# A two-mixer decoder trunk: the low parts of the second mixer's input weights made by another engine, and its inverse spread in other helpings

## The reference

```python
proj = h @ w_in
qkv, z, beta_logit, a_logit = jnp.split(proj, ...)
qkv = jax.nn.silu(causal_depthwise_conv(qkv, conv_w))        # four taps
q, k, v = jnp.split(qkv, ...); q = l2_norm(q) * dk ** -0.5; k = l2_norm(k)
decay_mat = jnp.exp(jnp.where(causal, g_i - g_j, -inf))      # g: cumulative log decay in a chunk
m = jnp.where(strict, (k * beta) @ k.T * decay_mat, 0.0)
u, w = triangular_solve(m, [v * beta, k * beta * exp(g)])    # unit lower triangular, 64 x 64
# then a scan over 16 chunks of 64 rows (and first the 16 meta rows) with state s
v_new = u - w @ s;  o = q_dec @ s + a_qk @ v_new;  s = s * tot + k_dec.T @ v_new
out = (rms_norm(o, head_norm) * silu(z)) @ w_out
```

## Time and profile before

| | us |
|---|---|
| median of 3 executions | 1534.98 |
| lowest and highest | 1532.82, 1536.03 |
| profiled execution, its own time | 1536.11 |
| span of its instructions | 1534.3 |

### The profile page before, as it was taken

The page is one execution under the profiler, slowest core; times in us unless marked ns, Lnnn a source line. Parts: engine busy times, 40 slices in busy tenths (PEclk is TensorE's granted clock), DMA queues, the critical chain, the costliest instruction groups (busy, mean ns, idle before and its releaser), DMA issues.

```text
span 1534.3 us, 21430 instructions
## 1 busy us (share of the span) xinstructions
PE 1444.4 (94%) x8490; PEld 1211.2 (79%) x8490; DVE 789.5 (51%) x1017; ACT 429.0 (28%) x914; POOL 381.4 (25%) x303
## 2 busy tenths in 40 slices
PE   6999999975999999999999989999998999999997
PEld 4777779973788779999999988978886667777775
DVE  4213612222444437654556799989933654444432
ACT  4322832103222214333332422212222531111111
POOL 3212123415111112221221221222343342222200
PEclk9999999997999999999999999999999999999998
DMA  5520214526645314345345232235359794555530
GB/s 186 176 83 28 98 55 125 160 105 228 191 166 171 121 55 115 92 113 137 101 118 197 70 84 72 70 97 179 109 189 240 199 253 135 147 148 155 155 83 28
DMA packets 213853, 200.81 MB, mean 131 GB/s; under 512 B 62840, under 2 KB 177032, under 8 KB 213504
## 3 DMA queue, kind: packets, MB, share of 16 engines
q1 hardware_dynamic: 207168, 187.99, 41.1%
q10 hardware_dynamic: 6592, 11.54, 2.8%
HBM read 132.39 MB, written 67.09 MB: 130 GB/s over the span
## 4 chain that ended last, share of the span: by engine, by line
PE 42%; DVE 13%; issue 3%; ACT 3%; DMA 2%; ACTq 0%; POOLq 0%; DVEq 0%; SPq 0%; POOL 0%
PE banks L2564 11%; PE banks L1898 11%; PE banks L1832 9%; DVE gdn L2102 6%; PE banks L2644 2%; PE banks L2612 2%; PE banks L2614 2%; DVE gdn L2099 1%; PE banks L1726 1%; DMA gdn<-in_gdn_w_out 1%; PE banks L1750 1%; PE banks L2630 1%; PE banks L2623 1%; DVE gdn L2107 1%; ACT gdn L1966 1%
## 5 line engine op out<-in xcount | busy, mean ns | idle before, releaser
L1832 PE MATMUL banks<-hn_hi,gdn 128*128 128x352 f32 x1488 | 303.6, 329 | 0.0
L1832 PEld LDWEIGHTS banks<-hn_hi,gdn 128*128 128x128 f32 x1488 | 243.9, 190 | 4.1 <-issue 2.7
L2077 POOL TENSOR_TENSOR gdn<-gdn,gdn 128x1024 fp32r<-128x1024 f32 x31 | 99.8, 3220 | 316.8 <-ACT gdn L1934 316.8
L2102 DVE SCALAR_TENSOR_TENSOR gdn<-gdn,conv_taps,gdn 128x1040 f32<-128x1040 f32 x96 | 162.2, 1689 | 3.4
L1898 PE MATMUL banks<-gdn,hn_hi 128*128 128x512 f32 x512 | 161.8, 396 | 0.4 <-DVE gdn L2109 0.4
L1832 PE MATMUL banks<-hn_lo,gdn 128*128 128x352 f32 x744 | 159.1, 322 | 0.0
L1832 PEld LDWEIGHTS banks<-hn_lo,gdn 128*128 128x128 f32 x744 | 126.7, 189 | 0.0
L1898 PEld LDWEIGHTS banks<-gdn,hn_hi 128*128 128x128 f32 x512 | 95.5, 188 | 26.3 <-issue 2.6
L750 PE MATMUL ai_p<-ai_whi,hn_hi 128*128 128x512 f32 x264 | 106.0, 402 | 5.5 <-DVE ai_wlo L575 2.5
L750 PE MATMUL ai_p<-ai_wlo,hn_hi 128*128 128x512 f32 x264 | 104.8, 397 | 0.0
L750 PE MATMUL ai_p<-ai_whi,hn_lo 128*128 128x512 f32 x264 | 104.3, 395 | 0.0
(11 more groups left out here) (287 smaller groups left out, 2477.1 us busy)
## 6 DMA issues: line engine op xcount, KB each, us to landing
gdn<-in_gdn_w_in SPq DMA_DIRECT2D x32, 512.0 KB, 4.1
ai_st<-in_gla_w_in SPq DMA_DIRECT2D x32, 256.0 KB, 4.7
gdn_kq<-gdn SPq DMA_DIRECT2D x16, 512.0 KB, 3.9
gdn_v<-gdn SPq DMA_DIRECT2D x16, 512.0 KB, 3.5
gdn<-in_gdn_w_in SPq DMA_DIRECT2D x32, 256.0 KB, 4.6
gdn<-gdn_kq SPq DMA_DIRECT2D x16, 512.0 KB, 3.7
gdn<-gdn_ek SPq DMA_DIRECT2D x16, 512.0 KB, 5.3
gdn<-gdn_v SPq DMA_DIRECT2D x32, 256.0 KB, 6.7
```

Source lines behind the costliest of these rows:

```text
L1832: last = pe.matmul(a[:, b, 0:m], w[n % 2][:, kt, :], x[:, kt, PAD + s:PAD + s + m], start=(kt == 0 and e == 0), stop=(kt == KT - 1 and e = ...
L2077: pool.tensor_tensor(lo[n % 2][:, :, :], st[n % 2][:, :, :], hi[n % 2][:, :, :].bitcast(F32), ALU.subtract).then_inc(S("ni_wlo"), 1)
L2102: dve.scalar_tensor_tensor(cv[:, :], xs[:, tap:tap + L], T.cw[:, tap, t:t + 1], cv[:, :], ALU.mult, ALU.add).then_inc(S("ni_conv"), 1)
```

## The change

Four edits. The low parts of tiles 4 to 32 are made by VectorE, in window n for tile n + 1, behind its other work of that window (for odd n up to 17 also behind both copies of `ev_k`) and ahead of the inverse; every wait on a low part of these tiles now counts `ni_wlo_v`. The preparatory work is cut up: the distances are done in windows 18 and 19, the exponents' second half (`differences`) moves from window 21 to 22, ScalarE's `exps` from window 22 to 23. The inverse begins in window 24, not 23, with a budget of 2800, not 4200. In the scan, the load of the second chunk's decay factors goes behind the first scan matrices, and 6 of the 16 fillers behind the meta products go ahead of them.

```diff
--- before.py
+++ after.py
@@ -1574,17 +1574,24 @@
                 return NQK + head_of_k(n) * P
             return 2 * NQK + v_of(n) * P
 
+        def lo_made(eng, n):
+
+            if n < 4:
+                wait(eng, S("ni_wlo"), n - 1)
+            else:
+                eng.wait_ge(S("ni_wlo_v"), n - 3)
+
         def sync(sp, ahead):
             def load(n):
                 wait(sp, S("ni_whi"), n - 3)
-                wait(sp, S("ni_wlo"), n - 3)
+                lo_made(sp, n - 2)
                 sp.dma_start(st[n % 2][:, :, :], wv[:, :, col(n):col(n) + P]).then_inc(S(f"ni_w_in{n % 2}"), 16)
 
             def load_z(p_):
                 if p_ < 4:
                     last = NIN - 2 + p_ // 2
                     sp.wait_ge(S("ni_whi"), last - 1)
-                    sp.wait_ge(S("ni_wlo"), last - 1)
+                    lo_made(sp, last)
                 elif p_ < NZ * KT - 4:
                     sp.wait_ge(S("ni_zhi"), p_ - 3)
                     sp.wait_ge(S("ni_zlo"), p_ - 3)
@@ -1817,7 +1824,7 @@
 
             def mm(n):
                 pe.wait_ge(S("ni_whi"), n - 1)
-                pe.wait_ge(S("ni_wlo"), n - 1)
+                lo_made(pe, n)
                 if n % 2 == 0:
                     wait(pe, S("ni_free0"), 3 * (n // 2))
                 else:
@@ -2039,7 +2046,7 @@
                     act.activation(sst[:, :], trA[0:NH * TT, 0, :], ACT.Copy).then_inc(S("ni_sse"), 1)
                 if n == v_tile(4):
                     logs()
-                if n == v_tile(5):
+                if n == v_tile(6):
                     exps()
 
             for n in range(NIN):
@@ -2084,7 +2091,7 @@
 
             for j in range(2):
                 pool.memset(tok[j][:, :, :], 0.0).then_inc(S("ni_tok_zero"), 1)
-            for n in range(2, NIN):
+            for n in range(2, 4):
                 split_lo(n)
             for p_ in range(NZ * KT):
                 z_lo(p_)
@@ -2101,6 +2108,11 @@
                     dve.wait_ge(S("ni_conv"), CONV * m + tap)
                     dve.scalar_tensor_tensor(cv[:, :], xs[:, tap:tap + L], T.cw[:, tap, t:t + 1], cv[:, :],
                                              ALU.mult, ALU.add).then_inc(S("ni_conv"), 1)
+
+            def split_lo(n):
+                dve.wait_ge(S("ni_whi"), n - 1)
+                dve.tensor_tensor(lo[n % 2][:, :, :], st[n % 2][:, :, :], hi[n % 2][:, :, :].bitcast(F32),
+                                  ALU.subtract).then_inc(S("ni_wlo_v"), 1)
 
             def tokens_out(buf, b, sem):
                 if b < 2:
@@ -2145,7 +2157,9 @@
                 b_ = be[:, half * L // 2:(half + 1) * L // 2]
                 dve.reciprocal(b_, b_).then_inc(S("ni_beta"), 1)
 
-            def distances():
+            HALVES = ((slice(0, 32), slice(0, C)), (slice(32, C), slice(32, C)))
+
+            def distances(n):
 
                 dve.wait_ge(S("ni_gs_in"), 48)
                 dve.wait_ge(S("ni_sct"), 3 * NH)
@@ -2153,10 +2167,12 @@
                     dve.wait_ge(S(f"ni_kq_out{j}"), 16 * NH)
                 gr = gs[:, 0:1, :]
                 gc = gs[:, 0, :].rearrange("p (j o) -> p j o", o=1)
-                for n, (r, c) in enumerate(((slice(0, 32), slice(0, C)), (slice(32, C), slice(32, C)))):
-                    form = [P, 32, c.stop - c.start]
-                    dve.tensor_tensor(dm_rows[:, r, c], bc(gc[:, r, :], form), bc(gr[:, :, c], form), ALU.subtract)\
-                       .then_inc(S("ni_dd"), 1)
+                r, c = HALVES[n]
+                form = [P, 32, c.stop - c.start]
+                dve.tensor_tensor(dm_rows[:, r, c], bc(gc[:, r, :], form), bc(gr[:, :, c], form), ALU.subtract)\
+                   .then_inc(S("ni_dd"), 1)
+                if n == 0:
+                    return
                 form = [NH, NMETA, NMETA]
                 dve.tensor_tensor(m_drows, bc(m_g[:, 0, :].rearrange("p (j o) -> p j o", o=1), form),
                                   bc(m_g[:, 0:1, :], form), ALU.subtract).then_inc(S("ni_dd"), 1)
@@ -2186,6 +2202,8 @@
                 dve.tensor_tensor(kd[:, 1, :], kd[:, 0, :], ln[:, 0, :], ALU.subtract).then_inc(S("ni_expo"), 1)
                 dve.tensor_tensor(kd[:, 0, :], kd[:, 0, :], ln[:, 0, :], ALU.subtract).then_inc(S("ni_expo"), 1)
                 dve.tensor_tensor(m_kd[:, :], m_kd[:, :], m_ln[:, :], ALU.subtract).then_inc(S("ni_expo"), 1)
+
+            def differences():
                 dve.wait_ge(S("ni_dd"), 3)
                 lr = ln[:, 0, :].rearrange("p (j o) -> p j o", o=1)
                 for r, c in ((slice(0, 32), slice(0, C)), (slice(32, C), slice(32, C))):
@@ -2289,15 +2307,19 @@
                 if h is not None:
                     ev_k(h, 0)
                     ev_k(h, 1)
-                if n == v_tile(2):
-                    distances()
+                if n in (v_tile(1), v_tile(2)):
+                    distances(n - v_tile(1))
                 if n == v_tile(3):
                     norms()
                 if n == v_tile(4):
                     exponents()
+                if n == v_tile(5):
+                    differences()
                 if n == v_tile(8):
                     scale_k()
-                left = 4200 if n >= v_tile(6) else 0
+                if 4 <= n + 1 < NIN:
+                    split_lo(n + 1)
+                left = 2800 if n >= v_tile(7) else 0
                 while left > 0:
                     left -= next(inverse)
             for b in range(3):
@@ -2514,9 +2536,9 @@
             load_meta()
             load_kt(0)
             load_kt(1)
-            load_ek(1)
             sp.wait_ge(S("ni_ua_out"), 16)
             load_ua(0)
+            load_ek(1)
             for n in range(2):
                 sp.wait_ge(S(("ni_zhi", "ni_zlo")[n]), KT * F.tiles // TT + 4)
             load_rows(0, 1)
@@ -2578,6 +2600,7 @@
                     mm.then_inc(S("ns_oT"), 1)
 
             def meta(fill):
+                fill(6)
                 pe.wait_ge(S("ni_zev"), F.tiles + 2)
                 pe.wait_ge(S("ns_in_m"), 96)
                 for hp, p, q in pairs():
@@ -2593,7 +2616,7 @@
                             hp = 2 * rnd + a
                             mm = pe.matmul(pS[rnd][p][:, a, :], ktm[RM[p], hp, :], vn[RM[p], hp, :], start=True, stop=True)
                     mm.then_inc(S("ns_mds"), 1)
-                fill(16)
+                fill(10)
 
             def plan(m):
```

## The result

| us | before | after |
|---|---|---|
| median (lowest to highest) | 1535.14 (1532.82 to 1536.03) | 1568.76 (1562.64 to 1573.44, 4 runs) |
| ratio to before, 95% interval | | 1.0219 [1.0180, 1.0258] |
| profiled execution, its span | 1536.11, 1534.3 | 1570.46, 1568.6 |
| granted clock over the span | 0.983 | 0.968 |

The change makes the kernel 2.2% slower, 33.6 us. The forecast was 1553, its range 1542 to 1563: the sign was right, the size was not, and the time lies 6 us above the range.

The account below looks back on a forecast made before the run. It took TensorE to have no slack in the key stage and the scan, and VectorE to hold it up in the value tiles. Terms: +14.3 +2.8 -14.5 +15 = +17.6 us, giving 1553 us, range 1542 to 1563.

Parts of the forecast that it names:

- The boundary of the key tiles: Key stage: TensorE waits 2.2 us for VectorE's low part at 8 boundaries, +17.7; with 3.4 returned, +14.3 us.
- a return of 0.43 per pair: Key windows: TensorE's small wait from GpSimd's subtraction colliding with VectorE's convolution goes, 0.43 us 8 times, -3.4 us.
- The clock: Key stage: 2 of the 8 stalls are followed by a fall of TensorE's clock, 1.4 us each, +2.8 us.
- The value tiles: Value stage: TensorE's waits for VectorE shrink from 18.2 to 4.7 us, with 1 more spared, -14.5 us.
- The end of the inverse and the scan's start: After the tiles: smaller helpings leave 23.4 us of inverse work, so the scan's first products start late, +15 us.
- TensorE, cold after such a gap, loses about 1: Scan's start: after the gap ahead of the first scan products TensorE loses about 1 us, counted within the +15.
- The slack: Before the scan: some 11 us between the landing of the inverse's loads and the scan's first products at 1153.33.
- The fillers: Scan's start: with 6 fillers ahead of the first products and 10 behind, 1.5 to 2 us come back.
- Rival A: Key stage: the clock falls at nearly all eight stalls, costing 11 us and not 2.8; 1561 us, chance 0.14.
- D: VectorE's taps: GpSimd's subtraction isn't what stretches them, so VectorE has 1.2 us more per tile; 1564 us, chance 0.05.
- B: Scan's start: its DMA-bound first stretch covers the late inverse, so the +15 falls to 0; 1538 us, chance 0.12.
- C: Key stage: VectorE's copies and subtraction finish before TensorE reaches the boundary, so no 2.2 us stall; 1528 us, chance 0.07.

Follow-up runs that it names:

- e5: The kernel after, but GpSimd makes the low parts up to tile 17 and VectorE those of tiles 18 to 32; 1554.0 us.
- e8: The kernel after, but VectorE makes each low part in two halves and TensorE waits for the second only ahead of the fifth of eight contraction steps; 1554.9 us.
- e12: The kernel after, but GpSimd makes all low parts again and the helping of the inverse is back at 4200; 1532.7 us.

## Why the prediction was wrong in size

**The boundary of the key tiles: right.** The stall was to be 2.2 us, eight times, and to be followed by a return of 0.43 per pair. Measured: eight standstills of 1.96, and a pair without a fall of the clock takes 29.65 us, forecast 29.7. In idle time, tiles 4 to 18 gained 13.9 us (11.9 to tile 17, 2.0 in tile 18), forecast 14.3. The estimate of the subtraction from the earlier trace rows, 1.2, is 1.22.

**The clock: the step that failed.** "I take 2 falls in 8, +2.8". There were 5 falls in 8, of 1.56 us: 7.8, some 5 more. The earlier trace rows had one fall after 2.45 us and none after 2.24, and I counted by nearness to two rows. The kernel before has more standstills of that size than the two, and I had left them out. One is this:

```profile
940.65 0.27 PE L1785 MATMUL banks<-consts,gdn 128*16 128x128 f32 x1 [2.36 <-DVE gdn L2107]
...
942.00:946.00 4.00, 4.00 (x21) 4.00 (x20) 3.93 (x6) 0.78 (x1) 0.00 (x0) 0.72 0.02 4
```

One of 2.59 us at 1175.5 was followed by a fall as well, one of 2.25 at 563.3 by none. With these, 3 of 5 were followed by a fall, which for eight would have been some 5. The price was small as well: the stretch from which I read 1.4 begins 0.5 us after the fall did. And the range took 0 to 6 for this term, though its bounds had been 0 and 11; the 7.8 lie between.

The clock had a second term, "TensorE, cold after such a gap, loses about 1", and it lost 2.9. For all other places it had none. Two more falls lie there. One is at the join of the two mixers, where TensorE stands still for 2.25 to 2.35 us in every kernel: it was followed by a fall in after, e5, e8 and e12 and not in the other nine, costs 3.0 us in after, and comes and goes with nothing that was edited. The other is behind tile 32's standstill: e8 has the same one (3.39) with no fall and a tile of 15.94, after has 17.09, so some 1.2 are clock. Together the clock made 5.0 + 1.9 + 3.0 + 1.2 = 11.1 of the 16.8 us that are missing in the profiled run.

The Trainium skill (TensorE: Matmul & The Clock Gate, section "HAM oscillation — how this bites in real kernels") describes a matmul kernel that waits some 3 to 5 us for a transfer once per tile and starts every tile at the lower clock. The standstills here are shorter: this case agrees for 17 of 32 of 1.96 us, and not for the eight of 1.43.

**The value tiles: right in place, 4 us too hopeful.** Forecast −14.5, measured −10.6. The waits at tiles 22 and 23 were to be 1.2 and are 1.5 (13.01 + 14.49 + 11.13 against three times 12.39), that of tile 31 was to be 1.8 and is 1.6. The miss is tile 32: forecast 1.7, measured 4.7, of which some 1.2 are the clock. Two splits of GpSimd's z weights start at 1001.68 and stretch two of VectorE's steps (128x256, 0.42 otherwise) to 1.39 and 1.40, so that its next copy is late by 2, and the standstill of 3.32 us at 1008.37 is followed by a lower clock. I had counted GpSimd as idle up to the last tile. The 1 us that a shorter backlog was to spare isn't there.

**The end of the inverse and the scan's start: right in kind, 5 us too small.** The work left over was to be +26.6 us to the end of the inverse (23.4 and 3.2 for the collisions) and is +28.4 against tile 32's copy. The last part, the meta tokens' small steps and the weighing, from 1146.56 in after and 1108.03 before, takes 24.7 and not 20.4, so the collisions add 4.3 and the work left over is 24.1. In after, six z splits stretch one step each by 1.0 to 1.15 (as 0.21 to 1.20) and GpSimd's product at 1163.09 one by 2.24, 8.4 in all, but the kernel before had 4.1 of that kind already. The slack, taken as 11, is 28.4 − 18.5 = 9.9. The fillers gave back 1.4 where the forecast had 1.5 to 2, and the clock took 2.9 and not 1. So the term comes to 18.5 − 1.4 + 2.9 = 20.0, and the profiles have 18.5 + 1.4 = 19.9; the forecast had 15.

The Trainium skill (SBUF — State Buffer, section "SBUF: two separate sides") has the shared ports as a lock for a whole instruction, and the forecast named it with 3 us more than it took itself. The trace agrees: the step at 1163.12 lasts 2.45 us beside a GpSimd product of 2.40 that began 0.03 before it.

**The range.** The four errors (+4.9 key stage, +3.9 value tiles, +4.9 end of the inverse and scan's start, +3.1 before tile 3) make 16.8, all of one sign. The last was read in one execution of after and may be luck; how much of it the median holds is not known. I had added the terms' bounds as if independent, but all four errors have a clock loss behind a standstill in them. Rival A, falls at nearly all eight (1561), was nearest in mechanism, with 5 of 8; D's time, 1564, lies nearer to 1568.8, but its mechanism is refuted. Rivals B, C and D fell: nothing of the late inverse was covered, no boundary was free of the stall, and without GpSimd the taps take 3.98 us for three in all tiles from 4 on.

## What to carry to other kernels

When work moves to another engine, its place in that engine's list decides more than its cost: the same 29 subtractions, eight of them behind two copies that wait for TensorE, cost 26 us more than with those eight ahead of the copies, where the move gains 6 to 10 us. A helping of background work that is made smaller saves next to nothing (2.2 us here) in windows that had room for it, and what it leaves over is paid where the result is due. A standstill near 2 us on TensorE had two prices here, its own and, in about half of the cases, a lower clock behind it; in the kernel that shortened it by 0.5 us the second was gone. A forecast should carry that second price at every standstill, and count all rows of the kernel before that bear on it.

## What I had not expected of the hardware

The clock's falls after standstills of 1.96 us: 17 in 32, 1.56 us each, and none in eight after 1.43, though neither the length of a standstill nor chance alone sorts all the places. The run-to-run spread goes with the clock: the four runs of after, from 1562.64 to 1573.44 us, have granted clocks of 0.973, 0.970, 0.968 and 0.964 in that order; the runs of before lie within 3.2 us. Behind a wait of 19 us the lower clock lasted from 4.9 to 14.5 us.

Small loads beside a large store: from the store of the small inverse to the first product that reads its neighbours, 14.9 us with 4 MB under way and 5.5 without.

A wait's name can mislead even where it is half of the whole loss: the list of waits gives 15.7 us in eight waits to ScalarE's L1941, and moving VectorE's L2114 alone made them vanish.
